# A hybrid attention block: index-stage slabs rounded in quarters, and the second norm's row factor moved behind the first feed-forward product

## The reference

```python
h = _rmsnorm(x, norm_mix[l])
proj = h @ w_in[l]
...
# indexer: rel = q_idx . k_idx * 32 ** -0.5, score = sum over 8 heads of w_idx * relu(rel), top_k(score)
...
merged = (jax.nn.sigmoid(g_sb) * (o_sb @ w_branch_sb[l])
          + jax.nn.sigmoid(g_sa) * (o_sa @ w_branch_sa[l]))
x = x + merged @ w_out[l]
h2 = _rmsnorm(x, norm_mlp[l])
x = x + jnp.square(jax.nn.relu(h2 @ w_ff1[l])) @ w_ff2[l]
```

## Time and profile before

| what | us |
|---|---|
| median of 3 runs (755.95 to 756.57) | 756.17 |
| profiled execution, its own time | 755.86 |
| its span | 753.8 |
| PE busy | 732.8 (97%) |
| DVE busy | 525.5 (70%) |
| ACT busy | 334.5 (44%) |
| POOL busy | 223.6 (30%) |

### The profile page before, as it was taken

How to read it: one execution, slowest core, us unless ns; L and a number is a source line. 1 busy time by engine, 2 the same in 40 slices (tenths; PEclk the granted TensorE clock), 3 DMA queues, 4 the chain that set the end, 5 groups by cost and what they waited for, 6 DMA issues and landing times.

```text
span 753.8 us, 9741 instructions
## 1 busy us (share of the span) xinstructions
PE 732.8 (97%) x3482; PEld 579.3 (77%) x3482; DVE 525.5 (70%) x730; ACT 334.5 (44%) x477; POOL 223.6 (30%) x193
## 2 busy tenths in 40 slices
PE   8999999989999999999999999999999999999998
PEld 4768778767777655678887888888888888888886
DVE  5354786698996866646664558787787969595972
ACT  5234644156664666852242344443525253524320
POOL 2113424200001455102121036362708081625610
PEclk9999999999999999999999999999999999999999
DMA  9307423310111212113163133324060514131102
GB/s 328 127 15 193 143 64 105 113 57 1 57 57 57 57 56 57 57 57 113 56 229 134 57 112 110 114 71 153 8 214 0 171 52 167 56 111 56 56 15 98
DMA packets 43893, 70.63 MB, mean 94 GB/s; under 512 B 2641, under 2 KB 27217, under 8 KB 43858
## 3 DMA queue, kind: packets, MB, share of 16 engines
q1 hardware_dynamic: 43858, 70.17, 28.4%
HBM read 65.71 MB, written 2.10 MB: 90 GB/s over the span
## 4 chain that ended last, share of the span: by engine, by line
PE 85%; DVE 7%; ACT 3%; POOL 2%; issue 1%; DMA 0%; DVEq 0%; SPq 0%; ACTq 0%; POOLq 0%
PE ps L1713 7%; PE ps L1711 7%; PE ps L1712 7%; PE ps L415 6%; PE ps L417 6%; PE ps L416 6%; PE ps L1739 6%; PE ps L1741 6%; PE ps L1740 6%; PE ps L408 5%; PE ps L410 4%; PE ps L409 4%; PE ps L1549 2%; DVE cut_lo L399 2%; PE ps L1593 1%
## 5 line engine op out<-in xcount | busy, mean ns | idle before, releaser
L1711 PE MATMUL ps<-b_hi,cut_hi 128*128 128x512 f32 (+1 forms) x272 | 102.6, 377 | 0.0
L1712 PE MATMUL ps<-b_lo,cut_hi 128*128 128x512 f32 (+1 forms) x272 | 102.4, 377 | 0.0
L1713 PE MATMUL ps<-b_hi,cut_lo 128*128 128x512 f32 (+1 forms) x272 | 102.4, 376 | 0.0
L415 PE MATMUL ps<-cut_hi,a_hi 128*128 128x512 f32 x224 | 90.0, 402 | 0.9 <-DVE a_lo L996 0.9
L417 PE MATMUL ps<-cut_hi,a_lo 128*128 128x512 f32 x224 | 87.6, 391 | 0.0
L416 PE MATMUL ps<-cut_lo,a_hi 128*128 128x512 f32 x224 | 87.4, 390 | 0.0
L399 DVE TENSOR_TENSOR cut_lo<-raw,cut_hi 128x2048 fp32r<-128x2048 f32 (+1 forms) x30 | 58.5, 1950 | 33.5 <-ACT cut_hi L391 33.5
L615 POOL TENSOR_TENSOR a_lo<-qo_sb,a_hi 128x512 fp32r<-128x512 f32 x49 | 78.2, 1629 | 5.6 <-ACT a_hi L874 5.6
L864 ACT ACTIVATE qo_sb<-ps 128x512 f32<-128x512 f32 x32 | 19.1, 598 | 136.4 <-PE ps L1713 91.8
L603 POOL TENSOR_SCALAR qo_sb<-qo_sb 128x128 f32<-128x128 f32 (+3 forms) x28 | 30.2, 1078 | 129.5 <-DVE snmax L1168 128.7
L391 ACT ACTIVATE cut_hi<-raw 128x2048 fp32r<-128x2048 f32 (+1 forms) x30 | 48.7, 1622 | 44.3 <-PE ps L410 22.7
(11 more groups left out here) (192 smaller groups left out, 1653.5 us busy)
## 6 DMA issues: line engine op xcount, KB each, us to landing
raw<-in_w_ff_dram SPq DMA_DIRECT2D x32, 1024.0 KB, 5.5
raw<-in_w_in_dram SPq DMA_DIRECT2D x16, 1024.0 KB, 5.3
gates<-in_x_dram SPq DMA_DIRECT2D x8, 512.0 KB, 7.2
raw<-in_w_out_dram SPq DMA_DIRECT2D x4, 1024.0 KB, 5.1
raw<-in_w_in_dram SPq DMA_DIRECT2D x4, 512.0 KB, 7.4
raw<-in_w_branch_sb_dram SPq DMA_DIRECT2D x2, 1024.0 KB, 5.0
raw<-in_w_branch_sa_dram SPq DMA_DIRECT2D x4, 512.0 KB, 6.1
out_dram<-gates SPq DMA_DIRECT2D x8, 256.0 KB, 2.0
```

Source lines behind the costliest of these rows:

```text
L415: nc.tensor.matmul(dst, l_hi, w_hi, start=start, stop=False)
L1711: T.matmul(dst, w_hi[:, w], b_hi[:, k, a:b], start=(k == 0), stop=False)
L1712: T.matmul(dst, w_hi[:, w], b_lo[:, k, a:b], start=False, stop=False)
L1713: mm = T.matmul(dst, w_lo[:, w], b_hi[:, k, a:b], start=False, stop=(k == KD - 1))
```

## The change

There are three edits.

1. In the index stage, `index_relus` and `index_scores` take a slab number: behind each of the four units of one part they cut a quarter of that slab. This places slab 5 between scores 0 to 3 on DVE, slab 6 between relus 12 to 15 on ACT and between scores 16 to 19 on DVE. DVE's cut of slab 3 moves from the end of group KVI to between the low parts of the indexer's queries in group QSB.
2. The second norm's DVE multiply takes only the gain, and waits for the add before it instead of POOL's row factor. The factor is put on the diagonal of four 128 x 128 tiles (DVE), PE multiplies the row of four with a tile of -1 into bank 4 (every partition then holds the factors of the 512 tokens), and ACT copies that, negated, to `token_r`.
3. DVE now empties the bank: `relu` is max(bank, 0) times `token_r` (L1269 in the new file), and ACT squares in place (`hidden_square`, L865). Each stands in its queue where that engine's step on the same slab stood before. PE waits for the relu where it waited for the square.

```diff
-            def index_relus(part):
+            def index_relus(part, cut=None):
...
                     A(rel[u % 2][:, 0:w], bank(6 + u % 2, 0, w), ACT.Relu, scale=IXD ** -0.5).then_inc(relu_done, 1)
+                    if cut is not None:
+                        act_cut(cut, u % 4, 4)
...
                         if g == KSB:
-                            index_relus(2 + m)
+                            index_relus(2 + m, 2 * g + 2 if m == 1 else None)
                         square(4 * g + m)
-                        if g == KSB and m == 1:
-                            act_cut(2 * g + 2)
...
-            def relu(n, c, first=False):
-
-                act.wait_ge(f1_done, 4 * n + c + 1)
-                if not first:
-                    act.wait_ge(s_made, 4 * (n - 1) + (3 if c % 2 == 0 else 4))
-                    act.wait_ge(l_lo, 7 * (n - 1) + (1 if c % 2 == 0 else 7))
-                A(hid[:, c, :], bank(6 + c % 2), ACT.Relu).then_inc(f1_relu, 1)
+            def hidden_square(n, c):
+
+                act.wait_ge(f1_relu, 4 * n + c + 1)
+                A(hid[:, c, :], hid[:, c, :], ACT.Square).then_inc(f1_sq, 1)
...
             f_high(0, 1)
-            relu(0, 0, first=True)
+            act.wait_ge(token_r_done, 1)
+            A(token_r[:, :], bank(4), ACT.Copy, scale=-1.0).then_inc(token_r_out, 1)
+            hidden_square(0, 0)
...
-            def index_scores(part):
+            def index_scores(part, cut=None):
...
+                    if cut is not None:
+                        dve_cut(cut, u % 4, 4)
...
                                         q_parts[0][:, :, t].bitcast(F32), ALU.subtract).then_inc(tr_out, 1)
+                        if m == 1:
+                            dve_cut(2 * KVI + 3)
                 if g == KSB:
                     dve.wait_ge(w_ready, 1)
-                    index_scores(0)
+                    index_scores(0, 2 * QSB + 3)
...
-                            index_scores(2 + m)
+                            index_scores(2 + m, 2 * g + 2 if m == 2 else None)
...
-                            if m == 1:
-                                dve_cut(2 * g + 2)
...
-                dve_cut(2 * g + 3)
+                if g not in (KVI, QSB):
+                    dve_cut(2 * g + 3)
...
-                    norm_scale(TB + m, xn2[m % 2], xres[:, m, :], mlp_gain)
+                    if m >= 2:
+                        dve.wait_ge(nt_done, 2 * (TB + m) - 2)
+                    dve.wait_ge(wo_out, TB + m + 1)
+                    V.tensor_tensor(xn2[m % 2], xres[:, m, :], mlp_gain, ALU.mult).then_inc(row_scaled, 1)
...
-            def square(n, c):
-                dve.wait_ge(f1_relu, 4 * n + c + 1)
-                V.scalar_tensor_tensor(out=hid[:, c, :], in0=bank(6 + c % 2), scalar=0.0, in1=hid[:, c, :],
-                                       op0=ALU.max, op1=ALU.mult).then_inc(f1_sq, 1)
+                    dve.wait_ge(row_ready, TB + m)
+                    V.tensor_scalar(token_diag[:, (m - 1) * P:m * P], ident[:, :], row_r[:, TB + m - 1:TB + m], None,
+                                    ALU.mult).then_inc(diag_made, 1)
+
+            def relu(n, c, first=False):
+                dve.wait_ge(f1_done, 4 * n + c + 1)
+                if not first:
+                    dve.wait_ge(s_made, 4 * (n - 1) + (3 if c % 2 == 0 else 4))
+                    dve.wait_ge(l_lo, 7 * (n - 1) + (1 if c % 2 == 0 else 7))
+                V.scalar_tensor_tensor(out=hid[:, c, :], in0=bank(6 + c % 2), scalar=0.0, in1=token_r[:, :],
+                                       op0=ALU.max, op1=ALU.mult).then_inc(f1_relu, 1)
...
-                pe.wait_ge(f1_sq, 4 * n + c - 1)
+                pe.wait_ge(f1_relu, 4 * n + c - 1)
...
             pe.wait_ge(nt_cut, 16)
+            pe.wait_ge(diag_made, TB)
+            T.matmul(bank(4), ones_f, token_diag, start=True, stop=True).then_inc(token_r_done, 1)
             ff1_part(0, 0, 256, S).then_inc(f1_done, 1)
```

More of the change, by code:

```diff
@@ L177, in block_kernel @@
         right = {A11: b11, S2: t2, A12: b21, S1: t1, S4: b22, S3: t3, A22: t4}
+        token_diag, token_r = qT_sa[:, 0, :], dist
         zsum = [slot(8), slot(9)]
@@ L249, in block_kernel @@
         row_scaled = sem("row_scaled")
+        diag_made = sem("diag_made")
+        token_r_done = sem("token_r_done")
+        token_r_out = sem("token_r_out")
         nt_done = sem("nt_done")
@@ L908, in _ @@
             f_high(0, 1)
-            relu(0, 0, first=True)
-            relu(0, 1, first=True)
+            act.wait_ge(token_r_done, 1)
+            A(token_r[:, :], bank(4), ACT.Copy, scale=-1.0).then_inc(token_r_out, 1)
+            hidden_square(0, 0)
+            hidden_square(0, 1)
             f_high(1, 0)
-            relu(0, 2, first=True)
+            hidden_square(0, 2)
             right_high(0, A11, first=True)
-            relu(0, 3, first=True)
+            hidden_square(0, 3)
             left_high(0, A11, first=True)
@@ L924, in act_round @@
                 f_high(g + 1, 1)
-                relu(g + 1, 0)
+                hidden_square(g + 1, 0)
                 for q in (S3, S4, A22):
@@ L931, in act_round @@
                     hidden_high(0)
-                relu(g + 1, 1)
+                hidden_square(g + 1, 1)
             def act_round_end(g):
@@ L938, in act_round_end @@
                 right_high(g, S3)
-                relu(g + 1, 2)
+                hidden_square(g + 1, 2)
                 right_high(g, A22)
                 right_high(g + 1, A11)
-                relu(g + 1, 3)
+                hidden_square(g + 1, 3)
                 left_high(g + 1, A11)
@@ L1319, in _ @@
             f_low(0, 1)
-            square(0, 0)
-            square(0, 1)
+            dve.wait_ge(token_r_out, 1)
+            relu(0, 0, first=True)
+            relu(0, 1, first=True)
             t1_t3(0, first=True)
@@ L1324, in _ @@
             f_low(1, 0)
-            square(0, 2)
+            relu(0, 2, first=True)
             right_low(0, A11)
-            square(0, 3)
+            relu(0, 3, first=True)
             def dve_round(g, first=False):
@@ L1332, in dve_round @@
                 right_low(g, A12)
-                square(g + 1, 0)
+                relu(g + 1, 0)
                 drain(g, A11, first)
@@ L1339, in dve_round @@
                 right_low(g, S4)
-                square(g + 1, 1)
+                relu(g + 1, 1)
                 drain(g, A12, first)
@@ L1348, in dve_round_end @@
                 t1_t3(g + 1)
-                square(g + 1, 2)
+                relu(g + 1, 2)
                 drain(g, S4, first)
@@ L1354, in dve_round_end @@
                 right_low(g + 1, A11)
-                square(g + 1, 3)
+                relu(g + 1, 3)
                 drain(g, A22, first)
@@ L1768, in pe_round @@
                 product(g, A22, first)
+            pe.wait_ge(token_r_out, 1)
             pe_round(0, first=True)
@@ L1777, in _ @@
                 if u in (4, 5):
-                    pe.wait_ge(f1_sq, 4 * (FG - 1) + u - 1)
+                    pe.wait_ge(f1_relu, 4 * (FG - 1) + u - 1)
                 else:
```

## The result

The changed kernel takes 758.02 us (median of 16 runs, 756.98 to 760.40) against 756.11 (16 runs, 755.77 to 756.57): a ratio of 1.003, 95% interval 1.0021 to 1.0038. It is slower by 1.9 us. The forecast was 757.0, with a range of 751.9 to 760.4. The profiled execution took 759.09 us, its span 757.4, at a mean granted clock of 0.995; that of the kernel before had 1.000.

The account below looks back on a forecast made before the run. The prediction took the kernel as one chain of TensorE matmuls, busy 732.8 of 753.8 us. 755.86 - 3.2 - 3.05 + 0.95 + 6.15 = 756.7, plus 0.31 for the median of the runs, gave 757.0, range 751.9 to 760.4.

Parts of the forecast that it names:

- Index stage, -3.2: Index stage: four TensorE stalls go, 0.8, 1.0 and 2.0 us, with 0.6 coming back at logits 21 to 23.
- Rival D: Index stage: quarters hold up relus and scores, most of the gain comes back, 2 us more, 759.0; chance 0.07.
- Second norm, -3.05: Second norm's transposes: TensorE's two waits, 1.74 and 1.31 us, go because the plain multiply needs nothing of ACT or POOL.
- f32 matmul, +0.95: Token matmul behind the second norm: one added f32 matmul of 512 columns costs 0.95 us, taken from record durations.
- Round 0, +1.6: First feed-forward round: the turned relu and square delay the drain of S1, so PE waits 1.6 us before S4.
- last round, +1.0: Last feed-forward round: S3's rounding stands behind a square and `last_high(0)`; the late drain of S1 costs 1.0 us.
- last hidden part, +2.3: Final products: VectorE's last relu comes late and ACT's square adds 0.6, so PE waits 2.3 us for POOL's low part.
- Rounds 1 to 5, +1.25: Feed-forward rounds 1 to 5: 41.1 us between POOL starts against 40.80; PE loses 0.25 a round, 1.25 us.
- Rival B: Feed-forward rounds: the coupling is hidden, 0 to 2 us lost, 750.8 to 752.8, say 751.7; chance 0.18.
- Rival C: Feed-forward rounds: DVE meets POOL more often, 1.1 us each, three times in six rounds, 760.3; chance 0.16.

Follow-up runs that it names:

- e8_whole: Kernel before with the index edit, but slabs 5 and 6 each cut whole behind the fourth unit instead of in quarters: 754.33 us, before 756.44.
- e3_turned: Kernel before with only relu on VectorE (times a row of ones) and square on ScalarE; norm and index stage unchanged, no token matmul: 763.07 us, ratio 1.009.
- e6_s3_first: Changed kernel with ScalarE's second square moved behind rounding the next slab and S3 (last round: behind S3's rounding too): 751.37 us, ratio to before 0.9943.
- e5_relu_first: Changed kernel with VectorE's last relu moved ahead of the last right operand's rounding and the four shared-sum adds: 755.04 us, before 756.44.
- e7_token_x3: Changed kernel with the float32 token matmul issued three times: median 760.90 us of five runs; a sixth took 1884.07.
- r2_at_end: Kernel before with index edit and plain norm multiply; relu and square keep their engines, squared row factor applied in the products' adds: 750.26 us, before 756.23.
- r2_again: Same kernel as r2_at_end, run again as partner of one with added filler matmuls: 749.75 us, before 755.86.

## Why the prediction was right, point by point

- **Index stage, -3.2.** Measured -3.25 in the changed kernel's trace, and 3.5 alone by the medians. Each of the four stalls had its size (idle time and a little), and 0.92 came back at the last logits against 0.6. Rival D (quarters hold up the scores, 2 us more than that 0.6) had the right mechanism, at 0.3 of its 2 us. What the prediction did not separate, e8_whole did: quarters matter for slab 6 only.
- **Second norm, -3.05.** Measured -3.21 by the starts, 3.45 alone by the medians.
- **f32 matmul, +0.95.** 0.86. The term was mis-sized by 0.1, by using durations where distances count.
- **Round 0, +1.6, last round, +1.0, last hidden part, +2.3.** Measured 1.56, 1.26 and 2.57. e3_turned shows that all three come from the turned order, e6_s3_first and e5_relu_first which queue entry makes which. That VectorE's relu of round 0 stood where the forecast left it (460.68, 4.87 earlier as all of TensorE there, against 465.67) has some luck in it: VectorE's rounding at 451.97 took 2.11 us where it had taken 1.22 (456.77), and the one at 459.54 took 1.21 where it had taken 2.31 (463.44). The forecast had neither.
- **Rounds 1 to 5, +1.25.** Measured 1.52: 0.16 in round 1 and 0.34 in each of the other four. The circle that the prediction worked out, S3's rounding late behind a square, VectorE's idle time used up, ScalarE's square between VectorE and GpSimd, 41.1 us from one GpSimd start to the next, is the one in the trace (41.14). e6_s3_first shows that S3's place is needed for it; that the square is needed too is argued from the trace and not tested. What was off is small: the loss is 0.34 a round and not 0.25.
- **Slab (1, 1), not foreseen, +0.19.** VectorE's low part of this slab (456.24, 3.38) ends at 459.62, and PE begins at 459.67, the first of its products 0.29 behind the matmul before instead of 0.23. e3_turned's trace has the same 0.2, so it belongs to the turned order.
- **Rival B (coupling hidden)** fell with e3_turned. **Rival C (longer round through meetings of VectorE and GpSimd)** has one new meeting a round in the changed kernel's trace, VectorE's instruction at 564.05, 1.87 us where e6_s3_first has 1.25; VectorE idles 2.87 us behind it, so it costs nothing.
- **What the forecast had not: the clock.** By the table the foreseen terms, the 0.19 and the start make 755.86 + 3.52 - 0.56 - 1.53 = 757.29, and the fastest run, at 0.999, took 756.98. The median is 0.7 to 1.0 above. The changed kernel's runs stand at 0.999 (756.98), 0.997 or 0.998 (757.2 to 758.6), 0.995 (759.1 to 759.6) and 0.993 (760.3, 760.4); before's, in the experiments, at 0.998 or 1.000 but for one at 0.997, about 0.5 us apart. The new last wait can bring a fall of its own: e3_turned's trace has a second low stretch of 3.41 us from 739.03 on, right behind its wait for the last hidden part, e5_relu_first's has none there. But e7_token_x3's trace has the same wait of 2.3 us and full clock, and kernels without the last wait (r2_at_end, e5_relu_first, e8_whole) have runs at 0.995 too, so a run's mean clock does not tell which wait it fell behind; only 0.993 was seen in the changed kernel alone. What decides in which execution the clock falls behind the same wait is left open.

So 757.0 was right by 1.0 us, with every foreseen wait in its place. The change was forecast at +0.8 and came to +1.9: the rounds cost 6.91 against 6.15, slab (1, 1) 0.19 against nothing, and the clock was not in the sum; 0.3 of this came back in the index stage, the norm and the token matmul.

## What to carry to other kernels

Where two engines pass a tile on, turning their order costs nothing by busy time, but everything queued behind the new second instruction inherits the first engine's place in its own queue: here 6.9 us in a kernel of 756, of which moving one ScalarE entry (and S3's rounding in the last round) took back 5.8. Look there first, and put what another engine waits for ahead of what nobody needs yet. Before moving a per-row factor behind a product, look whether it commutes to the last add, where the row is a partition and a scalar operand is nearly free. Compare starts of the same instruction in both traces; busy shares hid 0.34 us a round and all of the clock's cost.

## What the runs showed of the hardware

- Behind an idle stretch of TensorE of 3.0 us (and of 2.3 at the end) the granted clock was half (1.2 GHz) for 3.41 us, once for 6.83, in some executions and full in others of the same kernel (r2_again's trace has the fall, r2_at_end's has none). A fall of 3.41 us cost 0.5 to 0.6 us in attention, where a later wait takes part of it back, and 1.5 among the final products, where none does; the one of 6.83 us cost 1.7. With the idle stretch filled with matmuls four runs stood at a clock of 1.000 and one at 0.999.
- True f32 matmuls (128x128 by 512 columns) followed each other 0.86 us apart in e7_token_x3; their two records last 0.59 us each.
- An add of 128x512 floats with a row scalar out of PSUM took 741 ns, without the scalar 680.
